# Host-made columns of x and of the convolution's parameters in a two-layer decoder trunk

## What is computed

```python
h = x
for layer in range(DEPTH):                     # 2
    y = _rmsnorm(h, norm_mix_g[layer])
    h = h + _hybrid_mixer(y, w_in[layer], ...) # one product with w_in, then heads, then w_out
    y = _rmsnorm(h, norm_ffn_g[layer])
    h = h + (_swiglu(...) if layer % 2 == 0 else _moe_swiglu(...))
return _rmsnorm(h, norm_final_g)

# in the mixer
q_m, k_m, v_m, o_m, i_pre, f_pre, q_s, k_s, v_s = _split_columns(h @ w_in)
qk = _causal_conv_silu(concatenate([q_m, k_m]), conv_w, conv_b)   # 4 taps, per channel
# mLSTM heads from qk, v_m, the gates i and f, and o_m; stick-breaking attention from q_s, k_s, v_s
```

## Time and profile before

| | |
|---|---|
| median of 3 runs | 1443.39 us (1441.89, 1443.39, 1445.13) |
| profiled execution, span from the first to the last instruction | 1441.6 us |
| PE busy | 1425.0 us (99%) |
| DVE busy | 1151.2 us (80%) |
| ACT busy | 1004.7 us (70%) |
| POOL busy | 152.6 us (11%) |
| chain of work that ended last, by engine | PE 94%, DVE 3%, issue 2%, ACT 1% |
| DMA traffic over the span | 309 GB/s |

### The profile page before, as it was taken

The page is one execution under the profiler, slowest core; times in us unless marked ns, Lnnn a source line. Parts: engine busy times, 40 slices in busy tenths (PEclk is TensorE's granted clock), DMA queues, the critical chain, the costliest instruction groups (busy, mean ns, idle before and its releaser), DMA issues.

```text
span 1441.6 us, 20219 instructions
## 1 busy us (share of the span) xinstructions
PE 1425.0 (99%) x7609; PEld 1219.5 (85%) x7609; DVE 1151.2 (80%) x838; ACT 1004.7 (70%) x851; POOL 152.6 (11%) x199
## 2 busy tenths in 40 slices
PE   9999999999999999999999999999999999999997
PEld 8988999999988888888888888888888888888885
DVE  4677655555676888888988888888889888888897
ACT  5786543444887677777777777777777777777775
POOL 4100000000100599700000000000000000002000
PEclk9999999999999999999999999999999999999999
DMA  9843565554543699999999999999999999999993
GB/s 365 289 141 123 178 203 175 180 184 147 185 147 132 212 400 394 395 392 388 368 381 392 366 375 395 388 362 392 377 375 384 393 369 376 392 387 370 394 395 117
DMA packets 188147, 446.00 MB, mean 309 GB/s; under 512 B 7712, under 2 KB 9896, under 8 KB 188096
## 3 DMA queue, kind: packets, MB, share of 16 engines
q1 hardware_dynamic: 183232, 429.94, 81.6%
q0 software_dynamic: 3568, 11.62, 2.2%
q10 hardware_dynamic: 1296, 3.75, 0.6%
HBM read 434.79 MB, written 10.49 MB: 309 GB/s over the span
## 4 chain that ended last, share of the span: by engine, by line
PE 94%; DVE 3%; issue 2%; ACT 1%; DMA 0%; DVEq 0%; SPq 0%; ACTq 0%
PE ps L1647 88%; PE ps L2108 2%; ACT whi L679 1%; DVE wlo L1111 1%; PE ps L1682 0%; PE ps L2073 0%; PE ps L2044 0%; PE ps L1862 0%; DMA h<-in_x_dram 0%; PE ps L1739 0%; PE ps L2077 0%; PE ps L1660 0%; PE ps L1668 0%; PE ps L1741 0%; DVE y L1309 0%
## 5 line engine op out<-in xcount | busy, mean ns | idle before, releaser
L1111 DVE TENSOR_TENSOR wlo<-raw,whi 128x2048 fp32r<-128x2048 f32 x404 | 925.5, 2294 | 208.6 <-ACT whi L679 207.1
L679 ACT ACTIVATE whi<-raw 128x2048 fp32r<-128x2048 f32 x404 | 774.9, 1919 | 323.6 <-PE ps L1647 317.9
L1647 PE MATMUL ps<-whi,xT_hi 128*128 128x512 f32 x1056 | 417.9, 396 | 0.8 <-DVE wlo L1111 0.6
L1647 PE MATMUL ps<-wlo,xT_hi 128*128 128x512 f32 x1056 | 411.9, 390 | 0.0
L1647 PE MATMUL ps<-whi,xT_lo 128*128 128x512 f32 x1056 | 411.1, 389 | 0.0
L1647 PEld LDWEIGHTS ps<-wlo,xT_hi 128*128 128x128 f32 x1056 | 198.2, 188 | 42.4
L1647 PEld LDWEIGHTS ps<-whi,xT_hi 128*128 128x128 f32 x1056 | 198.3, 188 | 41.3 <-issue 2.0
L1647 PEld LDWEIGHTS ps<-whi,xT_lo 128*128 128x128 f32 x1056 | 198.6, 188 | 38.6
L1647 PE MATMUL ps<-whi,hid_hi 128*128 128x512 f32 (+1 forms) x536 | 210.7, 393 | 0.0
L1647 PE MATMUL ps<-wlo,hid_hi 128*128 128x512 f32 (+1 forms) x536 | 208.9, 390 | 0.0
L1647 PE MATMUL ps<-whi,hid_lo 128*128 128x512 f32 (+1 forms) x536 | 208.7, 389 | 0.0
(11 more groups left out here) (282 smaller groups left out, 905.5 us busy)
## 6 DMA issues: line engine op xcount, KB each, us to landing
raw<-in_moe_w_gate_dram SPq DMA_DIRECT2D x112, 1024.0 KB, 7.5
raw<-in_moe_w_up_dram SPq DMA_DIRECT2D x112, 1024.0 KB, 7.6
raw<-in_moe_w_down_dram SPq DMA_DIRECT2D x112, 1024.0 KB, 7.4
raw<-in_w_in_dram SPq DMA_DIRECT2D x27, 1024.0 KB, 5.4
raw<-in_ffn_w_gate_dram SPq DMA_DIRECT2D x10, 1024.0 KB, 5.2
raw<-in_ffn_w_up_dram SPq DMA_DIRECT2D x10, 1024.0 KB, 5.1
raw<-in_ffn_w_down_dram SPq DMA_DIRECT2D x10, 1024.0 KB, 4.8
raw<-in_w_out_dram SPq DMA_DIRECT2D x8, 1024.0 KB, 5.0
```

The source lines that it names most:

```text
L679: act.activation(whi[:, i % NSPLIT, :], raw[:, i % NRAW, :], ACT.Copy).then_inc(hi_ready, 1)
L1111: dve.tensor_tensor(wlo[:, i % NSPLIT, :], raw[:, i % NRAW, :], whi[:, i % NSPLIT, :].bitcast(F32), ALU.subtract).then_inc(lo_ready, 1)
L1647: ins = pe.matmul(acc, lhs, rhs, start=start and m == 0, stop=stop and m == 2, skip_group_check=True)
```

## The change

The host lays `x` out a second time, as columns: `x_columns[p, k, t] = x[t, 128 k + p]`, 1 MiB. It also lays conv_w and conv_b of both layers out as columns (`conv_columns`, 128 by 80 floats). For the first norm nothing is transposed on PE any more: the columns are loaded straight into `xT_f` (the same memory as `qkc`), ACT makes `xT_hi` and DVE `xT_lo` from it in SBUF. Block 0 (pieces 0 and 1) is loaded in halves, and the first half of piece 0 is split in two parts of 512 columns. x as rows (`h`) is still needed, for the squares and for the residual add, and is now loaded behind piece 2. The squares move on ACT behind the high split of piece 2. `token_scales` and `gates` move on PE, `rb_copy` on ACT and the evacuation of QS on DVE by one step of the loop in the first layer. `conv_parameters` and its copy are gone, POOL issues four loads fewer, ACT's queue one more.

```diff
-BEFORE_X, BEFORE_PIECE, BEFORE_CHOICE, BEFORE_SLOTS = 30, 44, 36, 8
+BEFORE_X, BEFORE_CHOICE, BEFORE_SLOTS = 58, 36, 8
...
@@ SyncE: order of the loads
-                        if (l, b, half) != (0, 0, 0):
+                        if (l, b) != (0, 0):
                             cols(n + 2 * b + half, w_in[l], half, FIRST_COLUMN[b])
+                        if (l, b, half) == (0, 1, 0):
+                            for t in range(TT):
+                                sp.dma_start(h[:, t, :], x[0, t * P:(t + 1) * P, :]
+                                             ).then_inc(x_in[t], 16)
...
+            first_columns(0, 0, 2)
+            first_rows_of(0, 0, half_in[0])
+            first_columns(1, 2, 4)
+            first_rows_of(0, 1, arrived[0])
+            first_columns(2, 4, 8)
+            first_rows_of(1, 0, half_in[1])
+            first_rows_of(1, 1, arrived[1])
             mixer(0)
...
@@ GpSimd
-                pool.dma_start(convrow[r0:r0 + CONV_K, :], conv_w[l]).then_inc(small_in, 16)
-                pool.dma_start(convrow[r0 + CONV_K:r0 + CONV_K + 1, :],
-                               conv_b[l:l + 1, :]).then_inc(small_in, 16)
...
@@ ScalarE, mixer of layer 0
+                    act.wait_ge(gT_in, 16)
+                    act.wait_ge(xc_in[0], 16)
+                    xT_high(0, 2)
+                    act.wait_ge(half_in[0], 16)
+                    high_part(0, 0, 512, first_hi)
+                    high_part(0, 512, 1024, first_hi)
...
+                    done[0] = 2
+                    split_upto(n + 2)
+                    act.wait_ge(wif_in, 16)
+                    act.activation(wif_hi[:], wif[:], ACT.Copy).then_inc(wif_hi_ready, 1)
                     square(s, 0)
                     square(s, 1)
...
@@ ScalarE, the loop over pieces
-                        if i == 1:
+                        if i == 2 - l:
                             rb_copy(s)
                         if i < 13:
                             split_upto(n + i + 3)
...
@@ VectorE, the loop over pieces
+                        if l == 0 and i == 2:
+                            evacuate(QS)
-                        if half == 1 and b in (QS, KS, QM, KM):
+                        if half == 1 and b in (QS, KS, QM, KM) and (l, b) != (0, QS):
                             evacuate(b)
                         if i < 13 and i not in (8, 10):
                             split_upto(n + i + 3)
...
@@ TensorE
-                if l == 0:
-                    for t in range(TT):
-                        transpose_h(s, 0, t)
-                    keep_busy(BEFORE_PIECE, 6)
...
-                    if half == 0 and two == 0:
+                    if half == 0 and two == 0 and s:
                         for t in range(TT):
                             transpose_h(s, 1, t)
...
-                        if i == 1:
+                        if i == 2 - l:
                             token_scales(s)
                             gates()
-                        if i == 1 and l == 0:
-                            conv_parameters()
```

More of the change, by code:

```diff
@@ L717, in hT_copy @@
             def hT_copy(s, half, to):
-                act.wait_ge(hT_ps, 4 * s + 2 * half + TT)
+                act.wait_ge(hT_ps, 4 * (s - 1) + 2 * half + TT)
                 for c in range(4):
@@ L866, in mixer @@
                             evacuate(b)
[L867 to L870, removed]
                         if i == 2:
@@ L1180, in mixer, with xT_low, low_part @@
                 if l == 0:
+                    def xT_low(k0, k1):
+                        for k in range(k0, k1):
+                            dve.wait_ge(hT_hi_ready, k + 1)
+                            dve.scalar_tensor_tensor(xT_lo[:, k, :], xT_f[:, k, :], gT[:, s, k:k + 1],
+                                                     xT_hi[:, k, :].bitcast(F32), ALU.mult,
+                                                     ALU.subtract).then_inc(hT_ready, 1)
+                    def low_part(i, c0, c1, ready):
+                        dve.tensor_tensor(wlo[:, i, c0:c1], raw[:, i, c0:c1],
+                                          whi[:, i, c0:c1].bitcast(F32), ALU.subtract
+                                          ).then_inc(ready, 1)
                     dve.wait_ge(gT_in, 16)
-                    hT_rest(s, 0)
+                    xT_low(0, 2)
                     dve.wait_ge(first_hi, 1)
-                    dve.tensor_tensor(wlo[:, 0, 0:PIECE // 2], raw[:, 0, 0:PIECE // 2],
-                                      whi[:, 0, 0:PIECE // 2].bitcast(F32), ALU.subtract
-                                      ).then_inc(first_lo, 1)
+                    low_part(0, 0, 512, first_lo)
+                    dve.wait_ge(first_hi, 2)
+                    low_part(0, 512, 1024, first_lo)
+                    xT_low(2, 4)
                     dve.wait_ge(hi_ready, 1)
[L1188 to L1195, removed]
+                    low_part(0, 1024, PIECE, lo_ready)
+                    xT_low(4, 8)
+                    dve.wait_ge(second_hi, 1)
+                    low_part(1, 0, 1024, second_lo)
+                    dve.wait_ge(hi_ready, 2)
+                    low_part(1, 1024, PIECE, lo_ready)
+                    done[0] = 2
+                    split_upto(n + 2)
                     dve.wait_ge(wif_hi_ready, 1)
@@ L1691, in first_columns_out @@
                 for two in range(2):
-                    if i == 0:
-                        pe.wait_ge((first_lo, lo_ready)[two], 1)
-                    for c in range(4):
-                        acc = ps[:, c // 2, 256 * (c % 2):256 * (c % 2) + 256]
-                        for k in (2 * two, 2 * two + 1):
-                            kk = 4 * half + k
-                            if c == 0:
-                                pe.wait_ge(hT_ready, 8 * s + kk + 1)
-                            ins = passes(acc, xT_hi[:, kk, :], xT_lo[:, kk, :],
-                                         hi[:, k, c * P:(c + 1) * P], lo[:, k, c * P:(c + 1) * P],
-                                         start=half == 0 and k == 0 and c % 2 == 0,
-                                         stop=half == 1 and k == 3, weights_move=False)
-                    if half == 0 and two == 0:
+                    both = (2 * two, 2 * two + 1)
+                    order = [(c, k) for c in range(4) for k in both]
+                    if i == 0 and two == 0:
+                        order = [(c, k) for k in both for c in range(4)]
+                    if i == 1:
+                        pe.wait_ge((second_lo, lo_ready)[two], (1, 2)[two])
+                    if (i, two) == (0, 1):
+                        pe.wait_ge(lo_ready, 1)
+                    for c, k in order:
+                        acc = ps[:, c // 2, 256 * (c % 2):256 * (c % 2) + 256]
+                        kk = 4 * half + k
+                        if c == 0:
+                            pe.wait_ge(hT_ready, 8 * s + kk + 1)
+                            if i == 0 and two == 0:
+                                pe.wait_ge(first_lo, k + 1)
+                        ins = passes(acc, xT_hi[:, kk, :], xT_lo[:, kk, :],
+                                     hi[:, k, c * P:(c + 1) * P], lo[:, k, c * P:(c + 1) * P],
+                                     start=half == 0 and k == 0 and c % 2 == 0,
+                                     stop=half == 1 and k == 3, weights_move=False)
+                    if half == 0 and two == 0 and s:
                         for t in range(TT):
```

85 lines of the change are left out of this document (46 added, 39 removed).

## The result

The changed kernel takes 1448.4 us (median of five runs, 1448.1 to 1448.8; a sixth run of 1573 us, at a mean granted clock of 0.848 where the others have 0.994 or 0.995, is left out), the kernel before 1443.7 us (median of six runs of the same comparison). The ratio is 1.0036, with a 95% interval from 1.0025 to 1.0046: 3.6 to 6.6 us slower. The profiled execution has a span of 1447.0 us against 1441.6, 5.4 us more. The forecast was 1446.9, so 3.5 us slower. Its direction and its mechanism are what happened; the size was 1.2 to 1.9 us short, because the loads of pieces 4 and 5 landed 1.8 and 1.0 us later than it had them.

A forecast was written before the change was run, and what follows sets the result against it. PE bounds the kernel, with an equally late ACT and DVE chain. Piece 5's low split at 38.7 us instead of 35.18 costs 3.5 us, PE's lead being worth nothing: 1443.4 becomes 1446.9 us, range 1443.2 to 1448.8.

The forecast's parts named there:

- the landing of pieces 4 and 5 in the queue of loads: SP's queue: 1 MiB more ahead of later pieces puts piece 4 at 33.3 us, piece 5 at 36.7.
- The step's own bounds: Loss of 2.8 us with piece 4 at 32.1 and the queue 0.6 quicker, 4.1 with piece 4 at 34.0.
- the rival of the clock: TensorE's clock falls in new waits before piece 3: about 1.5 us more, 1448.4 us; chance 0.10.
- Chain without slack: ACT and DVE up to `pair_sums`: it comes 19.4 us after piece 5's low split starts, whatever PE does.
- Start: First product on PE, needing no transposes of x: at about 6.95 us instead of 10.70, 3.75 us earlier.
- The lead: PE through piece 2, scales and gates: done at 28.0 us instead of 33.0, ahead by 5.0 us.
- its late bound: SP's queue: piece 4 lands at the latest 2.7 us before piece 5, at 34.0 us.
- The price of the path behind piece 4: From piece 4's landing: high split 1.95 us, low split 2.2, then 1.1 to the next DVE instruction; DVE free at 38.6.
- Two candidates for the start of the low split: Piece 5's low split starts at the later of DVE free, 38.6 us, and piece 5's high split done, 38.65.
- The share between the queues: POOL's and SP's queues alternate by packet; x's larger packets would bring piece 4 about 1 us before its latest time.
- The lead survives: Rival: loads land early, PE decides, and the full 5.0 us gain holds, 1438.4 us; chance 0.12 with the cases between.
- The chain gives some back: Rival: later in the mixer part of the loss returns, 1 to 2.5 us lost, 1445.1 us; chance 0.23.

The follow-up runs named there:

- e4: Kernel before with 1 MiB of x rows loaded additionally behind piece 2, overwritten unused: 1446.20 us, ratio 1.0026 to the kernel before.
- e1: Changed kernel with the rb copy on ACT and QS's evacuation on DVE back ahead of piece 4's splits: 1446.71 us, ratio 1.0028 to the kernel before.
- e2: Changed kernel with POOL's stores of zeros held back until piece 5 has landed: 1439.53 us, ratio 0.9977 to the kernel before.
- f2: Changed kernel with the columns of the first pieces in two loads of 512 KB instead of three: 1447.77 us, one run, no ratio.
- g2: Changed kernel with zeros held until piece 5 lands and the convolution's columns loaded from POOL's queue instead of ACT's: 1439.47 us, ratio 0.9977.
- g1: Changed kernel with two column loads of 512 KB instead of three and zeros held until piece 5 lands: 1438.23 us, ratio 0.9971.
- e3: Kernel before with only the stores of zeros held back until piece 5 has landed: 1442.43 us, ratio 1.0000.
- f4: Kernel before with the rb copy and QS's evacuation moved behind piece 4's splits: 1442.94 us, ratio 1.0000.

## Why the prediction was right, and where it failed

*The step that failed is the landing of pieces 4 and 5 in the queue of loads.* The forecast had them at 33.3 and 36.7 us; they landed at 35.1 and 37.7, so that the low split of piece 5 started at 40.38 us and not at 38.7. The two terms are taken apart below. The step's own bounds, 2.8 to 4.1 us, do not hold the measured 5.2; the time lies inside the stated range only since that was widened by the spread of the runs and by the rival of the clock, neither of which was the cause.

*Chain without slack: right.* The forecast took the low split of piece 5 as the point from which 19.4 us pass to `pair_sums`. After the change it is 59.79 less 40.38, 19.4 us; in e4 57.55 less 38.11, 19.4 us.

*Start: 1.0 us too early.* The first product comes at 7.98 us, not 6.95. The term that failed is the half piece: the sum let ACT go on from `xT_hi` at once, but its half landed at 6.5 us, where ACT's high part starts after 0.52 us of waiting; the columns of g came 0.2 us late as well. Two short waits for low parts (0.83 us inside piece 0, 0.48 us ahead of piece 2) add to it, so that the gates end at 30.57 and not at 28.0. This cost nothing, as the text said it would: PE then waited 2.99 us for piece 3. The lead going into that wait was 2.4 us instead of 5.0.

*Landing of pieces 4 and 5: the two terms.* The first is piece 5's 1.0 us: the step had assumed that what was piece 6's place would be reached at piece 6's time. By the bytes of SP's queue 0.4 us of it are a queue that is behind since its head, and 0.6 us are later loads that went ahead; the cause of both is open. The second is the choice of 33.3 for piece 4 where the range went up to 34.0, which is 2.7 us ahead of piece 5; it rested on a larger share for x's rows. The two pieces came 2.6 us apart: piece 4 was at its late bound. The reason was in the sum's own words: both ways all of POOL's bytes have gone by then. The last of the zeros land at 34.87 us, 0.2 us before piece 4, so no byte of theirs was left to move beside piece 5. Together, 1.0 plus 0.7 us, this is the 1.7 us from the forecast 3.5 to the measured 5.2. A smaller miss cost nothing: the zeros start at 12.81 us, 1.75 us earlier than before and not 2.1, and piece 3 still landed 0.5 us behind the latest time given for it, 28.6. The price of the path behind piece 4 was right: 33.3 plus 5.3 was 38.6 for DVE to be free, and 35.08 plus 5.30 is 40.38.

*Two candidates for the start of the low split.* In the forecast the branch through piece 4 (38.6) and that through piece 5 (38.65) were level. Measured, piece 5's high part ends at 39.62 and DVE is free at 40.38, so the branch through piece 4 decides, by 0.8 us. e1 takes that branch away and gains 0.9, of which 0.2 by an earlier landing.

*The share between the queues.* The two queues between 17 and 33 us in the changed kernel (packets, MB, share of 16 engines; q0 is POOL's, q1 SP's):

```profile
q0 software_dynamic: 1128, 4.04, 62.3%
q1 hardware_dynamic: 1185, 2.50, 40.3%
```

Packets are shared nearly evenly, as in rows 9, and SP's bytes rise from 2.29 to 2.50 MB in 16 us; the rows of x, in packets of 4 KB, are among them. That agrees with the rule of the Trainium skill that the forecast weighed (DMA: Bandwidth & Descriptors, Queues, rings and completion order). The result that was worked out from it, piece 4 1 us ahead of its late bound, did not come: a larger share for x's rows moves piece 4 only while zeros are left behind it, and there were none.

*Rivals.* "The lead survives" did not happen, but the condition given for it (zeros that don't crowd SP's queue, or come later) is what e2 makes true: piece 5 lands before 33.2, piece 4 before 29.9, and the kernel is 3 us faster than before. It keeps 2.9 us and not the 5.0 given, since the start was 1.0 us later and the short waits stayed. "The chain gives some back" is refuted: 5.18 us at 59.8 us are 4.84 at the last transposes, 0.34 us given back, where the rival left only 1 to 2.5 us lost. "TensorE's clock falls" is half right. After the 2.99 us of idling before piece 3 the products are 0.12 us apart, 2.4 GHz: no fall where it was forecast. It fell elsewhere, as PE's stretches show (stretch, length, busy and instructions, granted clock, share of the DMA engines, GB/s):

```profile
55.00:56.00 1.00, 1.00 (x9) 0.85 1.04 408
56.00:57.00 1.00, 1.00 (x7) 0.50 0.47 164
...
59.00:60.00 1.00, 0.94 (x7) 0.94 0.98 379
```

Between 55.7 and 59.1 us the clock is 1.2 GHz, and the 24 products in the chain above take 4.56 us where at 0.12 each they would take 2.9. That costs less than 0.1 us: the low soft part that `pair_sums` needs, at 58.68 us with a length of 0.96, ends at 59.64, and PE is done at 59.73. The 5.2 us do not come from the clock.

## What to carry over

An engine can be busy on the whole chain of waits while another chain arrives at the same time behind it; before a load is moved, follow that one back too, to the last link with a wait in it, and set that slack against the delay of each load behind the move. A megabyte ahead of the weights and early stores on another queue each cost nothing here and cost 3 us together, so a change to a load order is to be tried together with holding back the traffic that nobody waits for. Where two bounds of a landing time lie 2 us apart, ask which bytes are still to move when it lands: here that decided the bound. And before a difference between two executions is put down to an edit, compare the same landing in a run whose loads are unchanged: it moved by 0.2 us for piece 5 and by 1.1 us for piece 3.

## What the runs showed that was not expected

- **Equal packets, unequal bytes.** POOL's stores took 4.04 MB and SP's loads 2.50 MB in the same 16 us with 1128 and 1185 packets. With the stores held back (e2) nearly all goes to the loads, and pieces 4 and 5 land 8 us earlier.
- **A slow head.** In the first 1 to 8 us SP's queue moved 834 packets against 810 but 1.65 MB against 2.08 (rows above). Over half of the 0.43 MB is made up by 36.7 us; neither two column loads (f2) nor an emptier ACT queue (g2) removed the lag, and the cause is open.
- **The clock after short waits.** 2.99 us idle before piece 3: no fall. 1.78 us idle at 54.76, with the four small transposes behind it: 1.2 GHz from 55.7 to 59.1 us. In e4 two waits, 1.66 us before the gate transposes and 1.57 us before `pair_sums`, brought no fall at all. The Trainium skill (TensorE: Matmul & The Clock Gate, What's actually happening) says that the throttle follows how busy the engine has recently been; these rows agree that it is not the single wait that decides. In f2, where PE idled 2.50 us at the start, the 12 products from 9.08 us on ran 0.21 us apart; in g1, with 1.6 us idle at the same place, they ran at full speed.
- **A stretch at half clock near 470 us, in every trace.** The kernel before has it from 466.7 to 473.5 us, the changed one from 472.1 to 479.0, but e2 only for 3.4 us, from 466.3 on. It is as short in e3, e4 and f4, whose profiled executions, like e2's, have a mean clock of 0.997; in the nine other traces it is 6.8 us long, and the mean clock is 0.994 to 0.996. At half speed the 3.4 us between the two lengths are worth up to 1.7 us of a run. The 27 runs of the kernel before in the comparison of e1 to e4 lie in two groups in time, 12 from 1441.4 to 1442.2 us with a mean clock of 0.997 each, and 15 from 1443.0 to 1444.0, of which 14 have 0.995 or 0.996. That the length of this stretch makes the groups fits all this, and was not tried; the later comparisons have less sharply parted groups. If it is so, it is much of the spread of 2 to 3 us that hides small effects in this kernel. The 5.18 us at `pair_sums` lie ahead of the stretch and don't depend on it.
